# Six wide input products of a mixer: from fp32 to three passes of high and low parts, with modulation rows in two pieces between the low parts

## The chip, the cores and the metric

One core of a Trainium2 chip runs the whole program. The metric is the device time of one execution in microseconds. TensorE (PE; PEld is its weight load), VectorE (DVE), ScalarE (ACT), GpSimd (POOL) and SyncE (SP, which issues nearly all DMAs) run their own instruction streams and meet at semaphores.

## The reference, cut to what matters

The program is a long chain of transformer-like blocks on 256 tokens of width 1024. The change touches one stage, the input side of the first mixer (`even_mixer`):

```
sh, sc, g = adaln(c, e_mod_mix_w[j], e_mod_mix_b[j])
h = rmsnorm(x, e_norm_mix[j]) * (1.0 + sc) + sh
...
fq, fk, fv, ff, gq, gk, gv, gg, glr = jnp.split(h @ w_in, cuts, axis=-1)
...
sh, sc, g = adaln(c, e_mod_ffn_w[j], e_mod_ffn_b[j])
```

`h @ w_in` is (256 x 1024) by (1024 x 3096). Beside it the kernel computes modulation rows of later blocks, `silu(c) @ w + b`, from the same stream of weights.

## The kernel before

**Units.** Weights come in units: one unit is a set of two slots of the buffer `ring` (2 x 1 MB for 1024 rows by 2 x 256 columns) with two PSUM banks. There are three sets (`SETS`), used in turn. SP loads unit n only when `unit_done` says that unit n - 3 has been used by TensorE (`freed`), and it goes through the units strictly in order; the two loads of a unit end on `slot_full`.

**The stage `even_in`** has 13 units. Unit 0 is narrow (8 and 16 columns). Units 1, 3, 5, 7, 9, 11 (`MIX_AT`) are the six wide input units; I call them mix 0 to mix 5. Units 2, 4, ..., 12 (`EF_AT`) carry modulation weights; I call them mod 0 to mod 5. So mod i + 1 (unit 2i + 4) is loaded into the set that mix i (unit 2i + 1) leaves, and mix i + 2 into the set that mod i leaves.

**TensorE** goes mix 0, mod 0, mix 1, the small decay product, mod 1, mix 2, mod 2, and so on to mod 5. A mix unit is 32 fp32 matmuls of 128x128 weights by 256 columns (each is two records in the trace), by `wide` (L1269, output by column) or `tokens_first` (L1307, by token). A mod unit is only four one-column matmuls against ones (`mod_ef`, L1369), since VectorE has already multiplied the eight row blocks by silu(c) and added them (`products_in_place`, L3179 for the first, which waits for both slots of the unit, and L3182 for the other seven).

**ScalarE** copies each finished mix unit out of PSUM (`store` L2595, `store_tokens` L2609) and computes the soft gates. **VectorE** also turns the gates into decays (L3457 to L3471, then `raw` L3481).

**Products by parts.** Later stages already take fp32 products in three fp32r passes. ScalarE rounds the weights of a slot to fp32r in another place (`high_part`, L2460, one instruction for 128x2048, signals `w_high`); VectorE subtracts that from the slot and leaves the low part in the slot (`low_part`, L3298, `w_low`); TensorE then multiplies high by high, low by high and high by low (L1397, L1401 and L1405 in `even_ffn`, eight matmuls in each row, one record each). `half_done` says that the first slot of a unit has been used.

Of the kernel before, what the change touches and what calls it, by code (L numbers as in the profile page):

```python
# [13 lines left out]
P = 128  # L14
D = 1024
T = 256
# [53 lines left out]
def program(nc, A, out, stages=ORDER):  # L70
# [478 lines left out]
    def high_area(first, n):  # L549
        return store_area_r[:, first * T:(first + n) * T].rearrange("p (k t) -> p k t", t=T)  # L550
# [50 lines left out]

    EF_GATES = GU_UNITS if has("even_ffn") else 0
    AFTER_MOE = "ffn1_0" if has("moe") else None
# [92 lines left out]

    EVEN_SLOTS = 2 * GU_UNITS if has("even_ffn") else 0
    EVEN_H = KD if has("even_ffn") else 0

# [57 lines left out]
    with nc.Block() as block:  # L757
# [476 lines left out]
        def _(pe):  # L1234
# [148 lines left out]
            def even_ffn():  # L1383
                norm("ef")
                first = base["even_ffn"]

                def gate_up(u, i):
                    banks_free(u)
                    for s in range(2):
                        high, low = even_high(s), slot(u, s, KD, rounded=True)  # L1390
                        pe.wait_ge(w_high, 2 * i + s + 1)
                        for t in range(2):
                            out, cols = banks[2 * u.r + s][:, t * T:(t + 1) * T], slice(t * P, (t + 1) * P)
                            for k in range(KD):
                                if i == s == t == 0:
                                    pe.wait_ge(h_high, k + 1)
                                mm(out, high[:, k, cols], h_hi[:, k, :], start=(k == 0), stop=False)  # L1397
                            if t == 0:
                                pe.wait_ge(w_low, 2 * i + s + 1)
                            for k in range(KD):  # L1400
                                mm(out, low[:, k, cols], h_hi[:, k, :], start=False, stop=False)  # L1401
                            for k in range(KD):
                                if i == s == t == 0:
                                    pe.wait_ge(h_low, k + 1)
# [203 lines left out]
            def even_mixer():  # L1608
# [21 lines left out]
                mod_ef(1)  # L1630
                wide(Unit(first + MIX_AT[3]), KD, h)
                mod_ef(2)
                wide(Unit(first + MIX_AT[4]), KD, h)
                mod_ef(3)
                tokens_first(Unit(first + MIX_AT[5]), KD, by_token)
                mod_ef(4)
                wide(Unit(first + MIX_AT[6]), KD, h)
                mod_ef(5)
# [750 lines left out]
        def _(se):  # L2389
# [29 lines left out]
            def even_ffn():  # L2419
# [7 lines left out]
                for i in range(GU_UNITS):  # L2427
                    if i + 1 < GU_UNITS:
                        se.wait_ge(half_done, i + 1)
# [226 lines left out]
            def even_mixer():  # L2656
                input_in()
                norm("em")
                st = "even_in"
                se.wait_ge(cols_in, 16 * (len(COL_LOADS) + 3))  # L2660
                u = Unit(base[st])
# [15 lines left out]
                tally.wait(se)  # L2677
                activation(soft[:, 0:2, :], soft[:, 0:2, :], ACT.Ln, bias=ones[:, 0:1]).then_inc(soft_ready, 1)
                store(st, MIX_AT[3], lambda s: flat(fox_q[:, 2 * s:2 * s + 2, :]), scale=DH ** -0.5, with_ef=1)
                store(st, MIX_AT[4], lambda s: flat(fox_k[:, 2 * s:2 * s + 2, :]), with_ef=1)  # L2680

                se.wait_ge(query_raw, 1)
# [7 lines left out]
                for i in range(3):  # L2690
                    key(i)
                store_tokens(st, MIX_AT[5], fox_v, with_ef=1)
                store(st, MIX_AT[6], lambda s: flat(gla_g[:, 2 * s:2 * s + 2, :]), ACT.Silu, with_ef=1)
                for i in range(3, NB):
# [443 lines left out]
        def _(ve):  # L3138
# [49 lines left out]
            def even_low(i, s):  # L3188
                low_part(gate_unit(i), s, KD, even_high(s), 2 * i)

# [36 lines left out]
            def even_ffn():  # L3227
# [12 lines left out]
                for k in range(KD):  # L3240
                    ve.wait_ge(h_high, k + 1)
                    nc.vector.scalar_tensor_tensor(out=h_lo[:, k, :], in0=hT[:, k, :], scalar=shift(k), in1=as_f(h_hi[:, k, :]),
                                                   op0=ALU.add, op1=ALU.subtract).then_inc(h_low, 1)
# [195 lines left out]
            def even_mixer():  # L3439
                norm("em")  # L3440

                def products(i):
                    products_in_place(Unit(base["even_in"] + EF_AT[i]), mod_count(IN_MODS + i))

                products(0)
                ve.wait_ge(soft_ready, 1)
# [6 lines left out]

                products(1)
                ve.wait_ge(soft_ready, 2)
                x = gate_in[:, 0:2, :]
                tally.up(nc.vector.tensor_scalar(x, x, 0.0, None, ALU.min))  # L3457
                tally.wait(ve)
                tally.up(nc.vector.tensor_tensor(x, x, soft[:, 0:2, :], ALU.subtract))
                tally.wait(ve)  # L3460
                for j in range(2):
                    tally.up(nc.vector.tensor_tensor_scan(gla_b[:, j, :], ones[:, :], gate_in[:, j, :], 0.0, ALU.mult, ALU.add))
                tally.wait(ve)

                FLOOR = -60.0 * 16.0
                for j in range(2):
                    b = gla_b[:, j, :].rearrange("p (n t) -> p n t", t=GB)
                    tally.up(nc.vector.tensor_tensor(gla_qd[:, j, :].rearrange("p (n t) -> p n t", t=GB), b,
                                                     b[:, :, GB // 2 - 1:GB // 2].to_broadcast([P, NB, GB]), ALU.subtract))
                tally.wait(ve)  # L3470
                nc.vector.tensor_scalar(gla_qd[:, :, :], gla_qd[:, :, :], -FLOOR, None, ALU.min).then_inc(query_raw, 1)  # L3471
                products(2)
                products(3)

# [15 lines left out]

                for i in range(3):
                    raw(i)
# [724 lines left out]
```

## Time and profile before

| | us |
|---|---|
| median of 3 runs | 2916.94 (2914.49 to 2916.98) |
| the profiled execution, its own time | 2913.85 |
| its span, first to last instruction | 2912.1 |

The page gives PE busy 2800.3 us of the span, DVE 1945.6, ACT 1404.2 and POOL 278.3. An engine's busy time is a sum over the whole program, while the change lies in the first 5% of it, so the stage has to be read by itself: who waits there, and for what. The stage of the wide units runs from 48.6 to 142.0 us.

### The profile page before, as it was taken

The numbers are of one execution on the slowest core, as the hardware profiler recorded it, in microseconds if no ns is written. First come the engines' busy times: TensorE is split into PE (matmuls) and PEld (weight loads), VectorE is DVE, ScalarE is ACT, GpSimd is POOL, SyncE is SP. The second block draws the span as 40 slices with busy tenths as digits, with TensorE's granted clock in tenths as the row PEclk, the third lists the DMA queues.
The fourth block names the chain that finished last, engine by engine and source line by source line (L and its number), as shares of the span: only waits on it lengthen the run. The fifth ranks groups of instructions, "written<-read, shape, count | busy, mean of one in ns | idle before, by whom it ended". The sixth has DMA issues, their size and how long they took to land.

```text
span 2912.1 us, 39687 instructions
## 1 busy us (share of the span) xinstructions
PE 2800.3 (96%) x15590; PEld 2433.1 (84%) x15591; DVE 1945.6 (67%) x2310; ACT 1404.2 (48%) x1569; POOL 278.3 (10%) x248
## 2 busy tenths in 40 slices
PE   6999999989999999999998999999999999999999
PEld 5879988877888888888877888888888988996888
DVE  5466552548888888987544763785577577585765
ACT  2233323217777776776433551343555455435544
POOL 0015732300000000000001000002100010020000
PEclk8999999989999999999999999999999999999999
DMA  8836773368999999997553564333356456572553
GB/s 264 272 120 206 227 232 102 95 202 296 333 345 370 334 342 345 367 335 276 188 188 100 190 192 139 122 117 115 123 188 216 141 171 199 165 202 73 188 181 113
DMA packets 504828, 609.70 MB, mean 209 GB/s; under 512 B 50201, under 2 KB 371836, under 8 KB 504700
## 3 DMA queue, kind: packets, MB, share of 16 engines
q1 hardware_dynamic: 502224, 606.82, 62.8%
q8 instruction: 94, 1.54, 0.2%
q10 hardware_dynamic: 2476, 1.06, 0.1%
q14 instruction: 34, 0.28, 0.0%
HBM read 605.75 MB, written 1.05 MB: 208 GB/s over the span
## 4 chain that ended last, share of the span: by engine, by line
PE 83%; DVE 6%; DMA 4%; ACT 3%; issue 3%; POOL 1%; SPq 0%; DVEq 0%; ACTq 0%; POOLq 0%
PE bank L1452 14%; PE bank L2049 7%; PE bank L1456 7%; PE bank L1444 7%; PE bank L1895 4%; PE bank L1899 4%; PE bank L1908 4%; PE bank L1269 4%; PE bank L1808 3%; PE bank L1321 3%; PE bank L1957 2%; PE bank L1948 2%; PE bank L1949 2%; DMA ring<-in_o_exp_down 2%; PE bank L1401 1%
## 5 line engine op out<-in xcount | busy, mean ns | idle before, releaser
L3298 DVE TENSOR_TENSOR ring_r<-ring,store_area_r 128x2048 fp32r<-128x2048 f32 (+1 forms) x344 | 809.8, 2382 | 191.2 <-ACT store_area_r L2460 188.1
L2460 ACT ACTIVATE store_area_r<-ring 128x2048 fp32r<-128x2048 f32 (+1 forms) x344 | 670.9, 1974 | 229.1 <-PE bank L1456 57.2
L1452 PE MATMUL bank<-hT_sq_r,store_area_r 128*128 128x512 f32 x1376 | 347.9, 395 | 0.5 <-DVE ring_r L3298 0.5
L1452 PEld LDWEIGHTS bank<-hT_sq_r,store_area_r 128*128 128x128 f32 x1376 | 249.5, 190 | 45.8 <-DVE ring_r L3298 0.8
L2049 PE MATMUL bank<-hT,ring 128*128 128x256 f32 x1024 | 229.9, 380 | 0.0
L3757 DVE TENSOR_TENSOR ring_r<-ring,store_area_r 128x3072 fp32r<-128x3072 f32 x64 | 195.0, 3087 | 49.7 <-ACT store_area_r L2893 49.7
L2049 PEld LDWEIGHTS bank<-hT,ring 128*128 128x128 f32 x1024 | 190.8, 190 | 27.1 <-issue 3.1
L1456 PEld LDWEIGHTS bank<-hT_sq_r,ring_r 128*128 128x128 f32 x1376 | 187.9, 191 | 13.5
L2893 ACT ACTIVATE store_area_r<-ring 128x3072 fp32r<-128x3072 f32 x64 | 163.5, 2560 | 73.8 <-DMA ring<-in_o_exp_down 57.3
L1195 POOL TENSOR_TENSOR silu_g<-silu_g 128x768 f32<-128x768 f32 (+2 forms) x14 | 29.9, 2137 | 1707.2 <-ACT silu_g L2472 1338.2
L1456 PE MATMUL bank<-hT_sq_r,ring_r 128*128 128x256 f32 x1376 | 191.9, 282 | 0.0
L1895 PE MATMUL bank<-store_area_r 128*128 128x512 f32 x624 | 160.5, 399 | 4.1 <-issue 4.1
L1899 PE MATMUL bank<-store_area_r 128*128 128x512 f32 x624 | 155.1, 391 | 0.0
L1908 PE MATMUL bank<-ring_r,store_area_r 128*128 128x512 f32 x616 | 152.4, 389 | 0.0
L1899 PEld LDWEIGHTS bank<-store_area_r 128*128 128x128 f32 x624 | 117.9, 189 | 25.2
L1895 PEld LDWEIGHTS bank<-store_area_r 128*128 128x128 f32 x624 | 115.1, 190 | 28.0 <-issue 4.3
L1908 PEld LDWEIGHTS bank<-ring_r,store_area_r 128*128 128x128 f32 x616 | 115.2, 188 | 23.7
L1452 PE MATMUL bank<-act_both_r,store_area_r 128*128 128x512 f32 x528 | 126.2, 391 | 3.2 <-DVE act_both_r L3342 3.2
L1948 PE MATMUL bank<-store_area_r,act_r 128*128 128x512 f32 x308 | 122.4, 398 | 0.0
L1949 PE MATMUL bank<-store_area_r,act_r 128*128 128x512 f32 x308 | 120.3, 390 | 0.0
L3182 DVE SCALAR_TENSOR_TENSOR ring<-ring,csil 128x512 f32<-128x512 f32 x140 | 115.2, 823 | 4.9
L1452 PEld LDWEIGHTS bank<-act_both_r,store_area_r 128*128 128x128 f32 x528 | 97.0, 188 | 23.5 <-DVE act_both_r L3342 4.9
(563 smaller groups left out, 4774.4 us busy)
## 6 DMA issues: line engine op xcount, KB each, us to landing
ring<-in_o_exp_gate SPq DMA_DIRECT2D x88, 1024.0 KB, 7.2
ring<-in_o_exp_up SPq DMA_DIRECT2D x88, 1024.0 KB, 7.2
ring<-in_ffn_w_gu SPq DMA_DIRECT2D x88, 1024.0 KB, 6.6
ring<-in_o_exp_down SPq DMA_DIRECT2D x32, 1536.0 KB, 8.7
ring<-in_ffn_w_down SPq DMA_DIRECT2D x32, 1408.0 KB, 8.7
ring<-in_o_exp_down SPq DMA_DIRECT2D x32, 1280.0 KB, 11.5
ring<-in_ssd_w_in SPq DMA_DIRECT2D x32, 1024.0 KB, 7.2
ring<-in_e_mod_mix_w SPq DMA_DIRECT2D x12, 1024.0 KB, 9.2
```

Of the source, the lines that this page charges most:

```text
L1444: i = mm(out, w(k), x(k), start=(p == k == 0), stop=(p == 2 and k == blocks - 1))
L1452: mm(bank[:, :], w_hi(k), x_both(k), start=(start and k == blocks[0]), stop=False)
L1456: i = mm(bank[:, half * T:(half + 1) * T], w_lo(k), x_hi(k), start=False, stop=(stop and k == blocks[-1]))
L1895: mm(out, xg_r[:, k, HIGH], moe_cols(i, k, high_place(u)), start=(k == 0), stop=False)
L1899: mm(out, xg_r[:, k, LOW], moe_cols(i, k, high_place(u)), start=False, stop=False)
L1908: ins = mm(moe_out(banks[2 * u.r], i), xg_r[:, k, HIGH], moe_low(u, i, k), start=False, stop=(k == KD - 1))
L1948: mm(out, act_r[:, k, HIGH], high[:, j, :], start=(k == 0), stop=False)
L1949: mm(out, act_r[:, k, LOW], high[:, j, :], start=False, stop=False)
L2049: ins = mm(dense_bank(i, s)[:, half * T:(half + 1) * T], slot(u, s, KD)[:, k, half * P:(half + 1) * P], h(k), start=(k == 0), stop=(k == K ...
L2460: activation(dst, slot(u, s, kk), ACT.Copy).then_inc(w_high, 1)
L3298: nc.vector.tensor_tensor(slot(u, s, kk, rounded=True), slot(u, s, kk), as_f(high), ALU.subtract).then_inc(w_low, 1)
L3757: vec.tensor_tensor(down_wide(u, rounded=True)[:, j:j + m, :], down_wide(u)[:, j:j + m, :], as_f(down_high_wide(i)[:, j:j + m, :]), ALU.su ...
```

## The change

All six mix units take three passes instead of fp32 products: 96 fp32r matmuls each. ScalarE makes the high part of each slot (`high`, two per unit, and one of the inputs h), into `act` for slot 0 and the store area for slot 1. VectorE makes the low part of h and of each slot, and the modulation rows are cut in two pieces of four row blocks, laid between the two low parts of a unit (`lows`). The decays move behind the second low part of mix 2. The loads and their order are as before.

```diff
-    EVEN_SLOTS = 2 * GU_UNITS if has("even_ffn") else 0
-    EVEN_H = KD if has("even_ffn") else 0
+    MIX_SLOTS, MIX_H, MIX_HALVES = (12, KD, 6) if has("even_in") else (0, 0, 0)
+    EVEN_SLOTS = MIX_SLOTS + (2 * GU_UNITS if has("even_ffn") else 0)
+    EVEN_H = MIX_H + (KD if has("even_ffn") else 0)
...
+    mix_high = lambda s: high_area(56, KD) if s else act_r[:, 0:KD, :]
+    mix_lo = high_area(64, KD)
+    mix_unit = lambda i: Unit(base["even_in"] + MIX_AT[i + 1])
...
-                by_token = lambda k, a: hT[:, k, a * P:(a + 1) * P]
-                wide(Unit(first + MIX_AT[1]), KD, h)
+                def mix(i, tokens=False):
+
+                    u = mix_unit(i)
+                    banks_free(u)
+                    for s in range(2):
+                        high, low = mix_high(s), slot(u, s, KD, rounded=True)
+                        pe.wait_ge(w_high, 2 * i + s + 1)
+                        for t in range(2):
+                            out, part = banks[2 * u.r + s][:, t * T:(t + 1) * T], slice(t * P, (t + 1) * P)
+                            for p, (w, x) in enumerate(((high, h_hi), (low, h_hi), (high, mix_lo))):
+                                if p == 0 and i == s == t == 0:
+                                    pe.wait_ge(h_high, KD)
+                                if p == 1 and t == 0:
+                                    pe.wait_ge(w_low, 2 * i + s + 1)
+                                if p == 2 and i == s == t == 0:
+                                    pe.wait_ge(h_low, KD)
+                                for k in range(KD):
+                                    ins = mm(out, *((x[:, k, part], w[:, k, :]) if tokens else (w[:, k, part], x[:, k, :])),
+                                             start=(p == k == 0), stop=(p == 2 and k == KD - 1))
+                        ins.then_inc(unit_done if s else half_done, 1)
+                mix(0)
                 mod_ef(0)
-                tokens_first(Unit(first + MIX_AT[2]), KD, by_token)
+                mix(1, tokens=True)
                 pe.wait_ge(evac, first + 1)
                 pe.wait_ge(cols_in, 16 * (len(COL_LOADS) + 3))
                 for j in range(2):
                     i = mm(bank_x[:, j * T:(j + 1) * T], gla_w2[:, j * P:(j + 1) * P], soft[0:16, 2, :], start=True, stop=True)
                 i.then_inc(decay_ps, 1)
                 mod_ef(1)
-                wide(Unit(first + MIX_AT[3]), KD, h)
+                mix(2)
...
+                def high(i, s):
+                    if i >= 1:
+                        se.wait_ge(*((unit_done, mix_unit(i - 1).at(1)) if s else (half_done, i)))
+                    high_part(mix_unit(i), s, KD, mix_high(s))
+
+                se.wait_ge(h_ready, KD)
+                activation(h_hi[:, :, :], hT[:, :, :], ACT.Copy).then_inc(h_high, KD)
+                for s in range(2):
+                    high(0, s)
...
+                high(1, 0)
                 store(st, MIX_AT[1], lambda s: flat(gla_q if s == 0 else gla_k), with_ef=1)
+                high(1, 1)
+                high(2, 0)
                 store_tokens(st, MIX_AT[2], gla_v, with_ef=1)
+                high(2, 1)
...
+                def products(i, rows):
+                    products_in_place(Unit(base["even_in"] + EF_AT[i]), mod_count(IN_MODS + i), rows)
+
+                def lows(i, between=None):
+                    low_part(mix_unit(i), 0, KD, mix_high(0), 2 * i)
+                    products(i, range(KD // 2))
+                    low_part(mix_unit(i), 1, KD, mix_high(1), 2 * i)
+                    if between:
+                        between()
+                    products(i, range(KD // 2, KD))
+
+                ve.wait_ge(h_high, KD)
+                nc.vector.tensor_tensor(mix_lo, hT[:, :, :], as_f(h_hi[:, :, :]), ALU.subtract).then_inc(h_low, KD)
+                lows(0)
...
-                products(1)
-                ve.wait_ge(soft_ready, 2)
...
-                products(2)
-                products(3)
+                lows(1)
...
+                def decays():
+                    ve.wait_ge(soft_ready, 2)
+                    x = gate_in[:, 0:2, :]
...
+                lows(2, decays)
+                lows(3)
+                lows(4)
+                lows(5)
                 ve.wait_ge(query_exp, 1)
                 nc.vector.scalar_tensor_tensor(out=gla_qd[:, :, :], in0=gla_qd[:, :, :], scalar=DH ** -0.5, in1=gla_q[:, :, :],
                                                op0=ALU.mult, op1=ALU.mult).then_inc(query_ready, 1)
-                products(4)
-                products(5)
```

`high_part`, `low_part` and `products_in_place` are those described above; `EF_AT` gives the mod units.

Three places in the streams. First VectorE, from the gates' small instructions behind mod 0 on. Before, the eight instructions of mod 1 (here by their kind, 1 and 7) follow at once, then the decays:

```order
L3452 SCALAR_TENSOR_TENSOR store_area<-ones,store_area 8x256
L3179 TENSOR_SCALAR ring<-ring,csil 128x2x256
L3182 SCALAR_TENSOR_TENSOR ring<-ring,csil 128x2x256 x7
L3457 TENSOR_SCALAR store_area<-store_area 128x512
L3459 TENSOR_TENSOR store_area<-store_area 128x512
```

In the changed kernel, from the same instruction on, the rows are those of `lows(1)` (`ring_r<-ring,act_r` is the low part of slot 0, `ring_r<-ring,store_area_r` that of slot 1) and the beginning of `lows(2)`:

```order
L3505 SCALAR_TENSOR_TENSOR store_area<-ones,store_area 8x256
L3341 TENSOR_TENSOR ring_r<-ring,act_r 128x2048
L3222 TENSOR_SCALAR ring<-ring,csil 128x2x256
L3225 SCALAR_TENSOR_TENSOR ring<-ring,csil 128x2x256 x3
L3341 TENSOR_TENSOR ring_r<-ring,store_area_r 128x2048
L3225 SCALAR_TENSOR_TENSOR ring<-ring,csil 128x2x256 x4
L3341 TENSOR_TENSOR ring_r<-ring,act_r 128x2048
L3222 TENSOR_SCALAR ring<-ring,csil 128x2x256
```

The low part of mix 1's second slot now stands behind the first four product instructions of mod 1, the first of which (L3222) waits for both slots of the mod unit.

Second, TensorE between mod 0 and mod 1. Before:

```order
L1369 MATMUL bank<-ones,ring 128x1 x4
L1307 MATMUL bank<-ring,hT 128x256 x32
L1628 MATMUL bank<-store_area,gla_w 128x256 x2
L1369 MATMUL bank<-ones,ring 128x1 x4
```

In the changed kernel the first slot's six passes of mix 1 come first (they read alike but for `act_r` in place of `store_area_r`), and then these, the second slot's:

```order
L1642 MATMUL bank<-store_area_r,hT_sq_r 128x256 x8
L1642 MATMUL bank<-ring_r,hT_sq_r 128x256 x8
L1642 MATMUL bank<-store_area_r 128x256 x8
L1642 MATMUL bank<-store_area_r,hT_sq_r 128x256 x8
L1642 MATMUL bank<-ring_r,hT_sq_r 128x256 x8
L1642 MATMUL bank<-store_area_r 128x256 x8
L1651 MATMUL bank<-store_area,gla_w 128x256 x2
L1373 MATMUL bank<-ones,ring 128x1 x4
```

Of the second slot's 48 matmuls only the first eight (high by high) can run before the low part; the other 40 stand behind the wait for `w_low`.

Third, ScalarE around the copies of mix 0 and mix 1. Before they stood side by side:

```order
L2595 ACTIVATE store_area<-bank 128x512 x2
L2609 ACTIVATE store_area<-bank 128x2x256 x2
```

Now the high parts stand between them (`act_r<-ring` is slot 0, `store_area_r<-ring` slot 1):

```order
L2483 ACTIVATE act_r<-ring 128x2048
L2618 ACTIVATE store_area<-bank 128x512 x2
L2483 ACTIVATE store_area_r<-ring 128x2048
L2483 ACTIVATE act_r<-ring 128x2048
L2632 ACTIVATE store_area<-bank 128x2x256 x2
```

The high part of a unit's slot 0 is ahead of the copy of the unit before it, that of slot 1 behind it.

## Rows read from the trace of the kernel before

**Rows 1.** The page: busy time by engine, and the chain by engine.

```profile
PE 2800.3 (96%) x15590; PEld 2433.1 (84%) x15591; DVE 1945.6 (67%) x2310; ACT 1404.2 (48%) x1569; POOL 278.3 (10%) x248
...
PE 83%; DVE 6%; DMA 4%; ACT 3%; issue 3%; POOL 1%; SPq 0%; DVEq 0%; ACTq 0%; POOLq 0%
```

**Rows 2.** Busy time in the stage: PE, PEld, DVE, ACT, POOL, granted clock, DMA.

```profile
48.60:142.00 93.40, 90.42 (x437) 78.70 (x436) 39.87 (x63) 21.79 (x33) 0.00 (x0) 1.00 0.79 253
```

**Rows 3.** Timeline of PE: start, us, engine, line, [idle before <- releaser].

```profile
48.57 14.08 PE L1269 MATMUL bank<-hT,ring 128*128 128x256 f32 x64
...
63.30 14.06 PE L1307 MATMUL bank<-ring,hT 128*128 128x256 f32 x64
...
140.96 1.05 PE L1369 MATMUL bank<-ones,ring 128*128 128x1 f32 x8 [2.16 <-DVE ring L3182]
```

**Rows 4.** Waits of the stage: us in total, times, longest.

```profile
DVE ring L3179 <- DMA ring<-in_e_mod_ffn_w: 26.0, 3, 11.6
```

**Rows 5.** Timeline of SP's DMA issues.

```profile
62.69 1.26 SPq L766 DMA_DIRECT2D ring<-in_e_mod_mix_w  x2
63.99 4.18 SPq L766 DMA_DIRECT2D ring<-in_e_w_in  x2
...
93.35 1.26 SPq L766 DMA_DIRECT2D ring<-in_e_mod_ffn_w  x2
...
108.65 1.26 SPq L766 DMA_DIRECT2D ring<-in_e_mod_ffn_w  x2
...
124.12 15.96 SPq L766 DMA_DIRECT2D ring<-in_e_mod_ffn_w  x6
```

**Rows 6.** Timeline of DVE: the first product instruction of four mod units.

```profile
71.67 0.48 DVE L3179 TENSOR_SCALAR ring<-ring,csil 128x512 f32<-128x512 f32 x1 [16.87 <-DMA ring<-in_e_mod_mix_w]
...
103.07 0.49 DVE L3179 TENSOR_SCALAR ring<-ring,csil 128x512 f32<-128x512 f32 x1 [9.48 <-DMA ring<-in_e_mod_ffn_w]
...
117.27 0.49 DVE L3179 TENSOR_SCALAR ring<-ring,csil 128x512 f32<-128x512 f32 x1 [4.87 <-DMA ring<-in_e_mod_ffn_w]
...
134.90 0.49 DVE L3179 TENSOR_SCALAR ring<-ring,csil 128x512 f32<-128x512 f32 x1 [11.64 <-DMA ring<-in_e_mod_ffn_w]
```

**Rows 7.** Timeline of ACT: the last step of the inputs h.

```profile
38.84 3.30 ACT L2417 ACTIVATE hT<-hT,mods 128x256 f32<-128x256 f32 x8 [14.27 <-DVE hT L3167]
```

**Rows 8.** The critical chain in order of time: start, us, what.

```profile
39.49 9.16 PE bank L1619 x32
...
233.22 1.71 PE bank L1401 x8
...
238.80 0.96 PE bank L1397 x8
```

**Rows 9.** Groups by form, of `even_ffn` (first two) and of this stage.

```profile
L3298 DVE TENSOR_TENSOR ring_r<-ring,store_area_r 128x2048 fp32r<-128x2048 f32 x21 | 52.1, 2480 | 37.7 <-ACT store_area_r L2460 37.7
...
L2460 ACT ACTIVATE store_area_r<-ring 128x2048 fp32r<-128x2048 f32 x20 | 38.2, 1910 | 42.5 <-PE bank L1405 42.5
...
L3182 DVE SCALAR_TENSOR_TENSOR ring<-ring,csil 128x512 f32<-128x512 f32 x42 | 31.6, 752 | 1.5
...
L3179 DVE TENSOR_SCALAR ring<-ring,csil 128x512 f32<-128x512 f32 x5 | 2.4, 485 | 42.8 <-DMA ring<-in_e_mod_ffn_w 26.0 <-DMA ring<-in_e_mod_mix_w 16.9
```

**Rows 10.** Timeline of PE where it comes back from a wait.

```profile
229.94 3.29 PE L1397 MATMUL bank<-hT_sq_r,store_area_r 128*128 128x256 f32 x8 [3.57 <-ACT hT_sq_r L2415]
```

**Rows 11.** Windows around that wait: PE busy, granted clock, DMA share, GB/s.

```profile
228.00:230.00 2.00, 0.06 (x1) 1.00 1.10 348
...
234.00:236.00 2.00, 2.00 (x16) 0.78 0.66 210
...
236.00:238.00 2.00, 2.00 (x19) 1.00 0.01 2
```

**Rows 12.** Timeline of DVE: first and last step of the decays, and `raw`.

```profile
83.96 0.43 DVE L3457 TENSOR_SCALAR store_area<-store_area 128x512 f32<-128x512 f32 x1 [6.29 <-ACT store_area L2678]
...
87.25 0.43 DVE L3471 TENSOR_SCALAR store_area<-store_area 128x512 f32<-128x512 f32 x1
...
108.98 1.26 DVE L3481 TENSOR_SCALAR store_area<-store_area 128x128 f32<-128x128 f32 x6
```

More of the change, by code:

```diff
@@ L599, in ffn_gain @@
         return NORMS[name][1](k)
-    EF_GATES = GU_UNITS if has("even_ffn") else 0
+    EF_GATES = (6 if has("even_in") else 0) + (GU_UNITS if has("even_ffn") else 0)
     AFTER_MOE = "ffn1_0" if has("moe") else None
@@ L1390, in gate_up @@
                         high, low = even_high(s), slot(u, s, KD, rounded=True)
-                        pe.wait_ge(w_high, 2 * i + s + 1)
+                        pe.wait_ge(w_high, MIX_SLOTS + 2 * i + s + 1)
                         for t in range(2):
@@ L1395, in gate_up @@
                                 if i == s == t == 0:
-                                    pe.wait_ge(h_high, k + 1)
+                                    pe.wait_ge(h_high, MIX_H + k + 1)
                                 mm(out, high[:, k, cols], h_hi[:, k, :], start=(k == 0), stop=False)
                             if t == 0:
-                                pe.wait_ge(w_low, 2 * i + s + 1)
+                                pe.wait_ge(w_low, MIX_SLOTS + 2 * i + s + 1)
                             for k in range(KD):
@@ L1630, in even_mixer @@
                 mod_ef(1)
-                wide(Unit(first + MIX_AT[3]), KD, h)
+                mix(2)
                 mod_ef(2)
-                wide(Unit(first + MIX_AT[4]), KD, h)
+                mix(3)
                 mod_ef(3)
-                tokens_first(Unit(first + MIX_AT[5]), KD, by_token)
+                mix(4, tokens=True)
                 mod_ef(4)
-                wide(Unit(first + MIX_AT[6]), KD, h)
+                mix(5)
                 mod_ef(5)
@@ L2428, in even_ffn @@
                     if i + 1 < GU_UNITS:
-                        se.wait_ge(half_done, i + 1)
+                        se.wait_ge(half_done, MIX_HALVES + i + 1)
                         high(i + 1, 0)
@@ L2678, in even_mixer @@
                 activation(soft[:, 0:2, :], soft[:, 0:2, :], ACT.Ln, bias=ones[:, 0:1]).then_inc(soft_ready, 1)
+                high(3, 0)
                 store(st, MIX_AT[3], lambda s: flat(fox_q[:, 2 * s:2 * s + 2, :]), scale=DH ** -0.5, with_ef=1)
+                high(3, 1)
+                high(4, 0)
                 store(st, MIX_AT[4], lambda s: flat(fox_k[:, 2 * s:2 * s + 2, :]), with_ef=1)
+                high(4, 1)
                 se.wait_ge(query_raw, 1)
@@ L2691, in even_mixer @@
                     key(i)
+                high(5, 0)
                 store_tokens(st, MIX_AT[5], fox_v, with_ef=1)
+                high(5, 1)
                 store(st, MIX_AT[6], lambda s: flat(gla_g[:, 2 * s:2 * s + 2, :]), ACT.Silu, with_ef=1)
@@ L3188, in even_low @@
             def even_low(i, s):
-                low_part(gate_unit(i), s, KD, even_high(s), 2 * i)
+                low_part(gate_unit(i), s, KD, even_high(s), MIX_SLOTS + 2 * i)
             def mod_out(u, n, bank):
@@ L3240, in even_ffn @@
                 for k in range(KD):
-                    ve.wait_ge(h_high, k + 1)
+                    ve.wait_ge(h_high, MIX_H + k + 1)
                     nc.vector.scalar_tensor_tensor(out=h_lo[:, k, :], in0=hT[:, k, :], scalar=shift(k), in1=as_f(h_hi[:, k, :]),
@@ L3452, in even_mixer @@
                 tally.up(nc.vector.tensor_tensor_scan(fox_cum[0:8, 0, :], ones[0:8, :], x, 0.0, ALU.mult, ALU.subtract))
-                products(1)
-                ve.wait_ge(soft_ready, 2)
[L3456 to L3471, printed above, removed]
-                products(2)
-                products(3)
+                lows(1)
                 def raw(i):
@@ L3489, in key @@
                     nc.vector.tensor_tensor(kd, kd, gla_k[:, :, 0:w], ALU.mult).then_inc(key_ready, 1)
-                for i in range(3):
-                    raw(i)
+                FLOOR = -60.0 * 16.0
+                def decays():
+                    ve.wait_ge(soft_ready, 2)
+                    x = gate_in[:, 0:2, :]
+                    tally.up(nc.vector.tensor_scalar(x, x, 0.0, None, ALU.min))
+                    tally.wait(ve)
+                    tally.up(nc.vector.tensor_tensor(x, x, soft[:, 0:2, :], ALU.subtract))
+                    tally.wait(ve)
+                    for j in range(2):
+                        tally.up(nc.vector.tensor_tensor_scan(gla_b[:, j, :], ones[:, :], gate_in[:, j, :], 0.0, ALU.mult, ALU.add))
+                    tally.wait(ve)
+                    for j in range(2):
+                        b = gla_b[:, j, :].rearrange("p (n t) -> p n t", t=GB)
+                        tally.up(nc.vector.tensor_tensor(gla_qd[:, j, :].rearrange("p (n t) -> p n t", t=GB), b,
+                                                         b[:, :, GB // 2 - 1:GB // 2].to_broadcast([P, NB, GB]), ALU.subtract))
+                    tally.wait(ve)
+                    nc.vector.tensor_scalar(gla_qd[:, :, :], gla_qd[:, :, :], -FLOOR, None, ALU.min).then_inc(query_raw, 1)
+                    for i in range(3):
+                        raw(i)
+                lows(2, decays)
+                lows(3)
+                lows(4)
+                lows(5)
                 ve.wait_ge(query_exp, 1)
```

5 lines of the change are left out of this document (1 added, 4 removed).

## The prediction

> **What bounds the kernel now.** I read the page first: TensorE is busy for 96% of the span and the chain that ended last is TensorE for 83% [rows 1]. So time saved on TensorE counts, if nothing else takes its place in that stretch. Next the windows of the stage: from 48.6 to 142.0 us, 93.4 us, TensorE is busy for 90.42 and the granted clock is 1.00; VectorE is busy for only 39.87 and ScalarE for 21.79 [rows 2]. By busy time the stage is bound by TensorE, and there seems to be room for 12 low parts and 13 high parts.
>
> Then the timelines, to see who is close behind. A wide unit with its mod unit takes 14.7 us from start to start (48.57 to 63.30) [rows 3]. The loads of mod i + 1 are issued in the moment in which mix i ends: TensorE's first unit ends at 39.49 + 9.16 = 48.65 [rows 8], mix 0 at about 62.65, since SP issues at 62.69 [rows 5]. They have landed when VectorE's first product, which waited for them, starts: 62.69 to 71.67, 93.35 to 103.07, 108.65 to 117.27, 124.12 to 134.90 [rows 5, 6]. So a load takes 8.98, 9.72, 8.62 and 10.78 us. VectorE stands 26.0 us in three of these waits [rows 4]; today nothing that TensorE needs soon is queued behind it, except the modulation row itself. The eight products take 0.49 + 7 x 0.75 = 5.8 us [rows 9], and 9 to 11 + 6 us is just about the length of a mix unit: at the end TensorE waits 2.16 us for them [rows 3]. The view that decides is therefore not busy time but this ring: mix ends, load, VectorE, TensorE. It is as long as TensorE's own work already now.
>
> **The change part by part.**
>
> *Passes in place of fp32 products.* A mix unit takes 62.65 - 48.65 = 14.0 us now. Eight fp32r matmuls of the same shape take 0.96 us at full clock [rows 8], so 12 rows of eight take 11.5 us. By TensorE alone the six units would save 6 x 2.5 = 15 us, and the 3 us of waits with them if VectorE kept up.
>
> *High parts on ScalarE.* 1.91 us each [rows 9]. That of slot 1 waits until the unit before has ended and its copy, so it is there some 3 us after that end, while TensorE first works on slot 0 for 5.8 us. Nothing is late. Priced at nothing; were it exposed, it would be 1.9 us a unit.
>
> *Prologue.* h is ready at 38.84 + 3.30 = 42.1 [rows 7]. High part of h until 44.1, its low part until 46.5, low part of slot 0 until 48.9, four products until 51.7, low part of slot 1 until 54.1. TensorE needs the first at 48.65 + 1.0 and the last at 48.65 + 5.8 + 1.0 = 55.4. It is all under the narrow unit (9.16 us [rows 8]) and the first slot. Mix 0 then ends at 48.65 + 11.5 = 60.2, which is 2.5 us earlier than now.
>
> *Low parts and products in pieces on VectorE.* This is the step that counts. A low part took 2.48 us on average in the later stage [rows 9]; I take 2.4, as GpSimd, which is busy there, does nothing here [rows 2]. The order is: low part of slot 0, four products of mod i, low part of slot 1, four products. The first product waits for the mod unit's two slots, whose load is issued only when mix i - 1 ends. So the low part of slot 1 of mix i, on which 40 of the unit's 96 matmuls wait, now stands behind a load that starts when mix i - 1 ends. Counted from that end:
> - the load, for mod 1 to mod 5: 8.98, then for mod 2 the mean of the three like it (its own can't be read, VectorE came to it late), 9.1, then 9.72, 8.62, 10.78 [rows 5, 6]: 47.2 us, 9.44 on average;
> - four products, 0.49 + 3 x 0.75 = 2.8 us with small gaps [rows 9];
> - the low part, 2.4 us;
> - semaphores, 0.1 us;
> - 40 matmuls, 5 x 0.96 = 4.8 us at full clock [rows 8].
>
> TensorE meanwhile does mod i - 1, slot 0 and the first eight of slot 1: it stands still from about 1.0 + 5.8 + 1.0 = 7.8 us after the end to 14.7, for 6.9 us. What the clock does then shows where TensorE came back from a wait of 3.57 us at 229.94 [rows 10]: the granted clock was 1.00 at the end of the wait, and then eight matmuls took 1.71 us instead of 0.96, 0.214 each [rows 8]; it came back within the window from 234 to 236, of mean 0.78, so at about 234.9 [rows 11], after 5.0 us of work at the lower of the two levels, 1.2 GHz. For a wait of 6.9 us I take the same: 5.0 us at 0.214 are 23 matmuls, and 17 at 0.12 are 2.0, so the 40 take 7.0 us. Bounds: 4.8 (no fall) and 8.6 (all low). Behind them come slot 0 and more, whose clock doesn't matter: they have 6.9 us to spare.
>
> From one mix end to the next: 9.44 + 2.8 + 2.4 + 0.1 + 7.0 = 21.7 us, where the kernel before needs about 15.2 (mix 0 ends at 62.65; mod 5 starts at 140.96 after a 2.16 us wait, so mix 5 ended at 138.8 [rows 3]). Mix 5 ends at 60.2 + 5 x 21.7 = 168.9 and mod 5 at 170.0, against 140.96 + 1.05 = 142.0 now: **28 us later**.
>
> The Trainium skill ("TensorE: Matmul & The Clock Gate", HAM oscillation) says that bursts of matmuls parted by DMA waits each start at the low clock; it speaks against this change, and without that rule the sum would be 5 x 2.2 = 11 us less. For the load, the skill ("DMA: Bandwidth & Descriptors", Where 436 GB/s comes from, and Latency and other measured facts) gives about 358 GB/s and about 2 us of fixed cost, an estimate of 7.9 us for these 2.1 MB; by it the delay would be 20 us and not 28. The rows of this very stage are longer, and they decide.
>
> *Decays behind the low part of mix 2.* They last from 83.96 to 87.7, and six `raw` 1.26 us [rows 12], 5.0 in all, and the last four products of mod 2 come 3.0 us behind. So mod 2 is ready 8.0 us after that low part, and mix 2 ends 7.0 after it: mod 2 waits 1.0 us. That delays the start of mix 3, which has 6.9 us to spare, and not the load of mod 3, issued when mix 2 ends. Price nothing; without that cover 1 us. The weights of mix i + 2 are issued behind mod i and follow the mod loads by 1.3 us as now [rows 5]; even at twice 9 us after the end of mix i, the high part of slot 0 is done at 19.9 and the low part at 22.3, while TensorE wants them at 22.7 and 23.7, behind mix i + 1 and its mod unit. Not late either, though the low part by little.
>
> *After the stage* the order is as before: the end of mod 5 releases the same steps, later.
>
> **The sum.** 2913.85 + 28 = 2942 us against the profiled execution. Its time is 3.1 us below the median of the runs, 2916.94; I leave 2942. In it five periods cost 6.5 us each, 32.5 in all; the 2.5 us won at mix 0 and the last wait of 2.2 us, which goes away, are taken off.
>
> **The rivals.**
> 1. *The clock hardly falls in the waits.* For it: 7 us of standing still follow on 14 us of dense work. Against it: [rows 10, 11], a wait half as long. The tail is 4.8, a period 19.5, the delay 17 us: 2931. With the shortest load, 8.62, and a low part of 2.3 in all five: 18.6 a period, +12, 2926. Chance 0.17.
> 2. *The chain is slower yet.* All 40 matmuls at the low clock (8.6) and loads like the longest (10.78): 24.7 a period, +43, 2957. Either alone gives +36 (tail) or +35 (loads). Chance 0.12 for +33 and more.
> 3. *Faster: the load is hidden after all and TensorE bounds.* Then 48.65 + 6 x (11.5 + 0.9) + 1 for the decay product = 124 instead of 142: 18 us less, 2896. It decides at the landing: the low part would have to be done by 7.6 us after the mix end, so the load must land within 2.4 us of its issue. The shortest seen is 8.62. Chance 0.03.
> 4. *No change.* A period of 16.2 us (15.2, and a fifth each of the 2.5 won at the start and the 2.2 at the end) needs a landing within 3.9 us if the clock falls or 6.1 if it doesn't. Nothing in the rows speaks for it; it would also come about if the products' first wait didn't hold back the low part, and then the rival above takes over. Chance 0.03.
>
> **How the numbers follow.** The forecast's chance is 0.65, over 2934 to 2947. With the parts of rivals 1 and 2 that lie next to it, 2929 to 2952 leaves out the shortest loads without a fall of the clock, the far end of rival 2, and rivals 3 and 4: 2 in 10. Under 0.2% (6 us) a measurement of this kernel can't tell from no change. Faster 0.03, same 0.03, slower 0.94.
>
> **What the changed kernel's profile would show.** In the stage, about 28 us longer, TensorE's busy time stays at some 87 us (69 of passes, 11 of lost clock, 7 of the small ones), with five idle stretches of about 7 us, ended by VectorE's low part of slot 1 (L3341) on the matmuls of the second pass (L1642); none in mix 0. VectorE waits at L3222 for the DMA 6 us or more in each of five units, and the two loads before it are issued at each mix end. The granted clock is 0.5 behind each wait and returns within some 5 us. The passes take 0.96 us in dense stretches. If the loads landed well before VectorE came to L3222, or if TensorE's waits ended on ScalarE's high parts, the reasoning is wrong. The stages behind mod 5 should last as long as before.

## The result, and the profile after

| | us |
|---|---|
| before, median of 4 runs | 2915.72 |
| changed, median of 4 runs | 2936.84 (2935.41 to 2937.26) |
| ratio | 1.0074, 95% interval 1.0061 to 1.0088 |
| the changed kernel's profiled execution, its span | 2936.55, 2934.8 |

The changed kernel is 21 us slower, 0.7%. On its page TensorE is busy for less time than before, in a longer span (the chain has the same shares within a point) [rows 1]:

```profile
PE 2797.5 (95%) x15782; PEld 2440.1 (83%) x15783; DVE 1973.0 (67%) x2323; ACT 1427.6 (49%) x1582; POOL 279.2 (10%) x248
...
PE 84%; DVE 6%; DMA 3%; ACT 3%; issue 3%; POOL 1%; SPq 0%; DVEq 0%; ACTq 0%; POOLq 0%
```

The stage by windows (columns as in [rows 2]), now up to 166.0 us, which is 1.2 us short of its end:

```profile
48.60:166.00 117.40, 86.23 (x620) 84.20 (x620) 64.71 (x77) 37.91 (x40) 0.00 (x0) 0.85 0.61 197
```

117.4 us instead of 93.4, of which TensorE is busy for 86.2 instead of 90.4, and the mean granted clock is 0.85 instead of 1.00. So TensorE stands still for 31 us instead of 3. The waits of the changed kernel from 42 to 166 us say on what:

```profile
DVE ring L3222 <- DMA ring<-in_e_mod_ffn_w: 39.0, 4, 11.0
...
PE bank L1642 <- DVE ring_r L3341: 30.9, 5, 6.7
...
DVE ring L3222 <- DMA ring<-in_e_mod_mix_w: 9.4, 1, 9.4
```

Five waits of TensorE for a low part, 30.9 us in all; and ahead of each of them VectorE waits at the first product of a mod unit for its load. TensorE's timeline has all five: the first eight matmuls of slot 1, then the pass that needs the low part, with the idle time before it in brackets [rows 3]:

```profile
66.96 1.12 PE L1642 MATMUL bank<-store_area_r,hT_sq_r 128*128 128x256 f32 x8
74.76 2.07 PE L1642 MATMUL bank<-ring_r,hT_sq_r 128*128 128x256 f32 x8 [6.68 <-DVE ring_r L3341]
...
96.07 2.07 PE L1642 MATMUL bank<-hT_sq_r,ring_r 128*128 128x256 f32 x8 [5.92 <-DVE ring_r L3341]
...
117.67 2.08 PE L1642 MATMUL bank<-hT_sq_r,ring_r 128*128 128x256 f32 x8 [5.56 <-DVE ring_r L3341]
...
138.80 2.07 PE L1642 MATMUL bank<-ring_r,hT_sq_r 128*128 128x256 f32 x8 [6.36 <-DVE ring_r L3341]
...
159.68 2.08 PE L1642 MATMUL bank<-hT_sq_r,ring_r 128*128 128x256 f32 x8 [6.39 <-DVE ring_r L3341]
...
166.24 0.95 PE L1373 MATMUL bank<-ones,ring 128*128 128x1 f32 x8
```

One turn of the ring is best read in the chain (start, us, what). From the end of mix 0 to that of mix 1 it goes through SP, the load, four products, a low part and 40 matmuls:

```profile
60.50 0.55 SPq L770
...
61.10 8.46 DMA ring<-in_e_mod_mix_w
...
69.65 0.50 DVE ring L3222
...
72.50 2.21 DVE ring_r L3341
...
74.76 6.55 PE bank L1642 x40
81.33 0.55 SPq L770
```

This turn takes 20.8 us. The loads in all five turns, read as in [rows 5, 6] from the issue (60.50, 81.33, 103.76, 124.88, 145.72) to the first product, are 9.15, 9.63, 8.81, 8.82 and 8.86 us long. VectorE's rows for two of them:

```profile
69.65 0.49 DVE L3222 TENSOR_SCALAR ring<-ring,csil 128x512 f32<-128x512 f32 x1 [9.43 <-DMA ring<-in_e_mod_mix_w]
...
154.58 0.48 DVE L3222 TENSOR_SCALAR ring<-ring,csil 128x512 f32<-128x512 f32 x1 [10.61 <-DMA ring<-in_e_mod_ffn_w]
```

The windows around the first wait show the clock (TensorE's busy time stands behind the window's length, the granted clock behind that of all engines):

```profile
68.00:70.00 2.00, 0.07 (x1) 0.00 (x0) 0.35 (x1) 0.00 (x0) 0.00 (x0) 1.00 1.10 351
70.00:72.00 2.00, 0.00 (x0) 0.00 (x0) 1.89 (x4) 0.00 (x0) 0.00 (x0) 0.83 1.10 348
72.00:74.00 2.00, 0.00 (x0) 0.00 (x0) 2.00 (x2) 1.35 (x1) 0.00 (x0) 0.50 1.07 338
...
76.00:78.00 2.00, 2.00 (x11) 2.00 (x11) 1.93 (x4) 0.00 (x0) 0.00 (x0) 0.50 0.00 0
78.00:80.00 2.00, 2.00 (x18) 2.00 (x18) 1.93 (x1) 0.00 (x0) 0.00 (x0) 0.96 0.00 0
```

Its means put the fall at about 71.3, some 3 us into the wait, and the return at about 78.2, 3.4 us after the matmuls came back. Read in the same way, the return comes 6.0, 4.9, 4.2 and 3.8 us after the matmuls in the other four turns. Mod 5 ends at 166.24 + 0.95 = 167.2, 25.2 us later than before. At the end of the program 22.7 us of that are left (2934.8 against 2912.1).

### The profile page after: what moved, and what is told of

The parts are those of the page before. It is cut to its first block, busy times and chain, and to the rows that moved or that the text cites. A ratio compares the mean times of both kernels' runs of the same rounds, so it can differ in the third digit from the quotient of the medians.

```text
span 2934.8 us, 40109 instructions
## 1 busy us (share of the span) xinstructions
PE 2797.5 (95%) x15782; PEld 2440.1 (83%) x15783; DVE 1973.0 (67%) x2323; ACT 1427.6 (49%) x1582; POOL 279.2 (10%) x248
## 3 DMA queue, kind: packets, MB, share of 16 engines
HBM read 605.75 MB, written 1.05 MB: 207 GB/s over the span
## 4 chain that ended last, share of the span: by engine, by line
PE 84%; DVE 6%; DMA 3%; ACT 3%; issue 3%; POOL 1%; SPq 0%; DVEq 0%; ACTq 0%; POOLq 0%
PE bank L1456 13%; PE bank L2072 7%; PE bank L1460 7%; PE bank L1448 7%; PE bank L1918 4%; PE bank L1922 4%; PE bank L1931 4%; PE bank L1273 4%; PE bank L1325 3%; PE bank L1831 3%; PE bank L1980 2%; PE bank L1971 2%; PE bank L1972 2%; PE bank L1642 2%; DMA ring<-in_o_exp_down 1%
## 5 line engine op out<-in xcount | busy, mean ns | idle before, releaser
L3341 DVE TENSOR_TENSOR ring_r<-ring,store_area_r 128x2048 fp32r<-128x2048 f32 (+1 forms) x350 | 822.5, 2379 | 190.9 <-ACT store_area_r L2483 188.1
L2483 ACT ACTIVATE store_area_r<-ring 128x2048 fp32r<-128x2048 f32 (+1 forms) x350 | 682.2, 1973 | 229.3 <-PE bank L1460 57.1
L1199 POOL TENSOR_TENSOR silu_g<-silu_g 128x768 f32<-128x768 f32 (+2 forms) x14 | 29.9, 2134 | 1702.4 <-ACT silu_g L2495 1331.9
```

What stands on the lines that cost most here:

```text
L2483: activation(dst, slot(u, s, kk), ACT.Copy).then_inc(w_high, 1)
L3341: nc.vector.tensor_tensor(slot(u, s, kk, rounded=True), slot(u, s, kk), as_f(high), ALU.subtract).then_inc(w_low, 1)
```

## The experiments

All but half_mod_loads are compared with the kernel before by runs on the same chip. Where nothing else is said, an experiment is the changed kernel with one edit. "The stage ends" means the end of mod 5's matmuls: 142.0 us before, 167.2 in the changed kernel. A mod row is the few small matmuls of a mod unit, and the tail is the 40 matmuls of a mix unit behind the low part of its second slot.

**lows_first.** Both low parts ahead of the products.

```diff
 low_part(mix_unit(i), 0, KD, mix_high(0), 2 * i)
-products(i, range(KD // 2))
 low_part(mix_unit(i), 1, KD, mix_high(1), 2 * i)
 if between:
     between()
-products(i, range(KD // 2, KD))
+products(i, range(0, KD))
```

> Both low parts of a unit stand ahead of all eight products of its mod unit on VectorE; nothing else is changed. Theory A (the low part of slot 1 queued behind the products' wait for the load is what costs): TensorE no longer stands still inside a mix unit; what is left is the old ring, load 9.1 + eight products 5.9 + mod row 0.9 = 16 us from the end of one mix to the end of the mod row after the next, so that two units take about 27.5 us. The stage ends at about 131 to 137 us of the span instead of 167, and the time is 2900 to 2908 us, faster than both kernels. Rival B (the extra work of high and low parts on ScalarE and VectorE is too much whatever its order): the second slot still waits for its low part, and the time stays above 2925 us. Rival C (loads get longer when TensorE goes faster, the queue has more to do): loads of 12 us or more, time about 2915 us.

Measured: ratio 0.9985 (0.9975 to 0.9995), median 2910.17 us. The stage ends at 138.7. No matmul waits for a low part any more; what is left are waits of the mod rows for their products. TensorE's timeline of this kernel has them:

```profile
76.13 1.05 PE L1373 MATMUL bank<-ones,ring 128*128 128x1 f32 x8 [2.45 <-DVE ring L3225]
...
94.09 1.30 PE L1373 MATMUL bank<-ones,ring 128*128 128x1 f32 x8 [3.73 <-DVE ring L3225]
...
123.46 1.05 PE L1373 MATMUL bank<-ones,ring 128*128 128x1 f32 x8 [2.77 <-DVE ring L3225]
137.72 0.95 PE L1373 MATMUL bank<-ones,ring 128*128 128x1 f32 x8
```

The same instructions in another order end the stage 28.5 us earlier, and by the ratios the time is 24 to 26 us less. That is the mechanism of theory A; rival B needed over 2925 us, and rival C loads of 12 us or more (the mod loads that VectorE waited for took 8.7 to 9.8 us). Its numbers were too good: the stage ends at 138.7 and not at 131 to 137, and 2910.17 us lies outside 2900 to 2908. The longest wait is the one before mod 2, at 94.09, since the decays stand ahead of its eight products. VectorE itself waited there for ScalarE's gates, which come behind the high parts of mix 2:

```profile
83.23 0.43 DVE L3529 TENSOR_SCALAR store_area<-store_area 128x512 f32<-128x512 f32 x1 [2.75 <-ACT store_area L2715]
```

**one_ahead.** Only the first product, the one that waits for the load, ahead of the low part.

```diff
-products(i, range(KD // 2))
+products(i, range(1))
 low_part(mix_unit(i), 1, KD, mix_high(1), 2 * i)
 if between:
     between()
-products(i, range(KD // 2, KD))
+products(i, range(1, KD))
```

> Only the first product of each mod unit, which waits for its load, stays ahead of the low part of slot 1; the other seven go behind it. Theory A in its two parts (wait for the load, then what VectorE does before the low part): three products of 0.79 us leave the chain of each of five units, 5 x 2.36 = 11.8 us less, 2925 us, and TensorE still stands still for 3 to 4.5 us in each unit, ended by the low part; if that shorter wait leaves the clock up, up to 10 us more come off, 2915 us. Rival (only the number of instructions ahead of the low part counts, not the load): 2910 us or less, since 3 of 4 products are gone.

Measured: ratio 1.0035 (1.0020 to 1.0049), median 2923.71 us. The stage ends at 156.2, 11.0 us earlier than in the changed kernel, for 11.8 expected. TensorE waits 3.50 to 5.53 us in four of the units; in the fifth, mix 3, it doesn't wait for the low part, but mod 2 ahead of it waits 2.63 us for its products. The clock falls here too, so the 10 us more that it might have given back did not come: the first eight matmuls behind even the shortest of the four waits take 2.08 us, as behind a long one. The rival (2910 us or less) is out.

```profile
93.34 2.08 PE L1642 MATMUL bank<-hT_sq_r,ring_r 128*128 128x256 f32 x8 [3.50 <-DVE ring_r L3341]
```

**all_ahead.** All eight products ahead of it.

```diff
-products(i, range(KD // 2))
+products(i, range(8))
 low_part(mix_unit(i), 1, KD, mix_high(1), 2 * i)
 if between:
     between()
-products(i, range(KD // 2, KD))
```

> All eight products of a mod unit stand ahead of the low part of slot 1. Theory A (everything that VectorE does between the landing and that low part is on the chain): four more products of 0.79 us in each of five units, 15.7 us more, and some 1.6 us once at mix 0, where the low part now ends at about 57 us while TensorE wants it at 55.4: the stage ends at about 184 instead of 167 us and the time is 2953 us. Rival (the period is set by the load alone, VectorE has slack): 2937 us as before. With lows_first and one_ahead this gives a series in the number of products ahead: 0, 1, 4, 8.

Measured: ratio 1.0127 (1.0111 to 1.0143), median 2952.51 us. The stage ends at 186.1, 18.9 us later than with four ahead, for 17.3 expected, and mix 0 now has a wait too, of 1.83 us. TensorE's other five waits grow to 9.15 to 10.96 us:

```profile
80.41 2.08 PE L1642 MATMUL bank<-ring_r,hT_sq_r 128*128 128x256 f32 x8 [10.96 <-DVE ring_r L3341]
```

The series of 0, 1, 4 and 8 products ahead gives stage ends of 138.7, 156.2, 167.2 and 186.1 us. The first product alone, 0.5 us of work and one wait, costs 17.5 us; the other seven together 29.9.

**half_mod_loads.** Half the bytes in each mod unit (the second edit is shown by what it comes to, the choice of the row block).

```diff
 for s, src in enumerate(mod_columns(IN_MODS + EF_AT.index(at))):
-    load(u, s, src)
+    load(u, s, src[:, 0:KD // 2, :])
...
-nc.vector.scalar_tensor_tensor(out=w(0), in0=w(k), ...
+nc.vector.scalar_tensor_tensor(out=w(0), in0=w(1 + (k - 1) % 3), ...
```

> The mod units of this stage load only the first four of eight row blocks (half the bytes), and the products take rows 1 to 3 again in place of 4 to 7, so the modulation rows made from them are other numbers; instructions and waits are as many. Later stages that depend on these rows can take another time, so the stage itself is read. Theory A (the load's own length is on the chain): a load takes about 6 instead of 9.05 us and the stage ends some 5 x 3 = 15 us earlier, at about 152 us instead of 167. Rival (VectorE's own work sets the period, and the load only seems to be waited for): the end stays at 165 to 167 us.

Measured: the stage ends at 146.5, 20.7 us earlier. The loads take 6.25, 5.35, 5.48, 5.30 and 5.24 us, 3.5 less each, which is 17.7 in five turns. SP's and VectorE's timelines for the second:

```profile
78.99 0.92 SPq L770 DMA_DIRECT2D ring<-in_e_mod_ffn_w  x2
```

```profile
84.34 0.49 DVE L3222 TENSOR_SCALAR ring<-ring,csil 128x512 f32<-128x512 f32 x1 [6.78 <-DMA ring<-in_e_mod_ffn_w]
```

Most of the other 3 us come from mix 2: its wait for the low part is only 1.64 us, the matmuls behind it ran at full rate, and its tail took 5.1 us instead of 7.67. Behind the wait of 3.78 us they ran slowly from the start. Behind those of 2.84 and 2.78 us only the first eight ran at full rate; then the clock fell, and these tails took 6.55 us, hardly less than the 6.90 and 6.72 of the changed kernel.

```profile
72.39 2.07 PE L1642 MATMUL bank<-ring_r,hT_sq_r 128*128 128x256 f32 x8 [3.78 <-DVE ring_r L3341]
...
89.45 1.22 PE L1642 MATMUL bank<-hT_sq_r,ring_r 128*128 128x256 f32 x8 [1.64 <-DVE ring_r L3341]
...
122.25 1.22 PE L1642 MATMUL bank<-ring_r,hT_sq_r 128*128 128x256 f32 x8 [2.84 <-DVE ring_r L3341]
123.30 1.64 PE L1642 MATMUL bank<-store_area_r 128*128 128x256 f32 x8
```

So the load's length is on the chain, and its rival is out. In four of the five turns TensorE still waits for the low part behind it; in mix 3 it doesn't, as mod 2 ahead of it waits 2.78 us for its own products. One execution was taken of this one, and its whole time isn't compared.

**filled_wait.** 48 spare matmuls where TensorE stands still.

```diff
 if p == 1 and t == 0:
+    if s == 1 and i > 0:
+        for n in range(6 * KD):
+            mm(bank_sum[:, T:2 * T], high[:, n % KD, 0:P], h_hi[:, n % KD, :], start=(n == 0), stop=(n == 6 * KD - 1))
     pe.wait_ge(w_low, 2 * i + s + 1)
```

> The changed kernel with 48 spare matmuls of 128x128 by 256 (into unused columns of a bank) behind the first eight matmuls of slot 1 in mix 1 to mix 5, in the time in which TensorE stands still. Theory A with the clock term as in the prediction: the spare work is hidden, the granted clock stays at 1.00, the 40 matmuls take 4.8 us instead of the 6.5 to 7.7 measured, 10 to 11 us less in the five units: 2926 us. Rival (the clock behind a wait costs nothing that counts, or VectorE holds up the later passes too): 2937 us as before. Rival (spare work isn't hidden): 5 x 5.8 us slower, 2966 us.

Measured: ratio 1.0069 (1.0050 to 1.0089), median 2932.49 us. By its whole time it can't be told from the changed kernel, whose two ratios are 1.0074 and 1.0068, so the stage has to decide. It ends at 162.7, 4.5 us earlier, not 11. The tails went as expected: in all five units the granted clock is 1.00 behind the spare work, the passes start 0.96 us apart (the first two 1.05), and the tail takes 5.0 to 5.1 us, about 10 us less in all. In mix 1, where the wait is longer than the spare work, that work is hidden too:

```profile
67.64 5.92 PE L1640 MATMUL bank<-hT_sq_r,store_area_r 128*128 128x256 f32 x48
75.09 1.22 PE L1645 MATMUL bank<-ring_r,hT_sq_r 128*128 128x256 f32 x8 [1.53 <-DVE ring_r L3344]
76.14 1.12 PE L1645 MATMUL bank<-store_area_r 128*128 128x256 f32 x8
...
101.90 1.87 PE L1373 MATMUL bank<-ones,ring 128*128 128x1 f32 x8 [2.34 <-DVE ring L3228]
...
112.47 5.92 PE L1640 MATMUL bank<-hT_sq_r,store_area_r 128*128 128x256 f32 x48
118.23 1.12 PE L1645 MATMUL bank<-hT_sq_r,ring_r 128*128 128x256 f32 x8
```

The rest was given back at mod 2 and mix 3, whose turn takes 23.6 us instead of 21.1. With mix 2's tail shorter, mod 2 has to wait for its products behind the decays (2.34 us, at 101.90), and mix 3 starts late and at the low clock. VectorE came to the products at 108.22 there, so with 5.1 us for four of them and the low part its low part was ready at 113.3, but the spare work lasts until 118.2: 4.9 us of it are exposed. So the clock term stands, read at the five tails; for the whole time the run was too blunt, its filler being of one length.

**hidden_work.** 4.6 us more for VectorE in each of five units, ahead of the landing.

```diff
 low_part(mix_unit(i), 0, KD, mix_high(0), 2 * i)
+if i:
+    for n in range(4):
+        tally.wait(ve)
+        tally.up(nc.vector.tensor_tensor(std[:, :], flat2(hT[:, 0:4, :]), flat2(hT[:, 4:8, :]), ALU.subtract))
 products(i, range(KD // 2))
```

> The changed kernel with four spare subtractions of 128x1024 (about 1.15 us each, 4.6 us, into a scratch tile) on VectorE between the low part of slot 0 and the first product in units 1 to 5, in the time in which it waits for the load. Theory A (only what stands behind the landing counts): nothing changes, 2937 us, as VectorE waits 6.5 to 11 us there. Rival B (VectorE has too much to do in this stage): 5 x 4.6 = 23 us slower, 2960 us.

Measured: ratio 1.0071 (1.0054 to 1.0088), median 2935.48 us, against 2934.65 for the changed kernel on the same chip (next). The added work came to 5.0 us in each unit. VectorE's wait for the load is shorter by it (11.04 us at this place in the changed kernel), and the stage ends at 168.2, which is 1.0 us later than in the changed kernel's first profile and 2.3 later than in its second:

```profile
92.35 0.48 DVE L3222 TENSOR_SCALAR ring<-ring,csil 128x512 f32<-128x512 f32 x1 [6.07 <-DMA ring<-in_e_mod_ffn_w]
```

25 us of extra work cost about 1 us of the median, within the spread of the runs, while in all_ahead 15.7 us moved between the landing and the low part cost 18.9 us of the stage. That settles rival B: it isn't the amount of work on VectorE.

**changed_again.** The changed kernel once more.

> The changed kernel itself, on the same chip as the others of this call: 22 us slower than the fp32 kernel, the stage's end at 167 us within 1 us, under every theory. It gives the spread of the loads (8.8 to 9.6 us) and of the clock's return from one chip to the next.

Measured: ratio 1.0068 (1.0052 to 1.0084), median 2934.65 us, which is 18.7 us slower than the kernel before and not 22; the stage ends at 165.8, so it is 1.4 us off the first profile and a little outside the 1 us expected. The loads take 8.6 to 9.8 us. One changed kernel against itself thus differs by about 1.4 us in the stage, and smaller differences between experiments say nothing.

**lows_first_decays_later.** As lows_first, with the decays between the two low parts of mix 3.

```diff
 low_part(mix_unit(i), 0, KD, mix_high(0), 2 * i)
-products(i, range(KD // 2))
+if between:
+    between()
 low_part(mix_unit(i), 1, KD, mix_high(1), 2 * i)
-if between:
-    between()
-products(i, range(KD // 2, KD))
+products(i, range(KD))
...
-lows(2, decays)
-lows(3)
+lows(2)
+lows(3, decays)
```

> Both low parts ahead of all eight products, as in lows_first, and the decays moved from mix 2 (where the mod row came 3.7 us late behind them) to mix 3, between its two low parts. Theory A (VectorE's order around the landing sets the rest): the 3.7 us wait before mod 2 goes and none takes its place, the stage ends at about 135 us, some 7 us before that of the fp32 kernel; ratio to it 0.9975 to 0.998, and 3 to 4 us faster than lows_first. Rival (the ring load + products + mod row gives the time back at the next mod row): stage end at 138.7 as in lows_first, ratio 0.9985.

Measured: ratio 0.9968 (0.9955 to 0.9981), median 2907.1 us against 2915.91 of the kernel before: faster than both kernels. The stage ends at 137.2 instead of 138.7. So the gain over lows_first in the stage is 1.5 us and not 3.7, no more than the spread just named: the wait before mod 2 is gone, but two later mod rows wait for their products, where only one did:

```profile
76.32 1.86 PE L1373 MATMUL bank<-ones,ring 128*128 128x1 f32 x8 [2.56 <-DVE ring L3225]
...
105.97 1.05 PE L1373 MATMUL bank<-ones,ring 128*128 128x1 f32 x8 [2.15 <-DVE ring L3225]
...
135.80 1.41 PE L1373 MATMUL bank<-ones,ring 128*128 128x1 f32 x8 [2.37 <-DVE ring L3225]
```

That is in part the rival of its expectation. Of its 9 us in the whole time the stage accounts for 4.8; where the others are isn't shown, and the interval of its ratio reaches down to 5.5 us.

## Why the prediction was right

It said 2942 (2929 to 2952) and slower; measured are 2936.84. As a difference it said 28 us, and 21.1 were measured: the forecast was built on an execution of 2913.85, 1.9 us below the median that counts, and that hides a part of the miss. The profiled executions differ by 25.2 us at the stage's end and by 22.7 at the last instruction. The five waits, their line, their releaser and their absence in mix 0 came as listed. By its steps:

- **The ring.** Right, and shown in both directions: without the product that waits ahead of the low part the slowdown is gone (lows_first), with more products ahead it grows (all_ahead), and the load's length counts in full (half_mod_loads).
- **Load.** 9.44 us expected, 9.05 measured on average: 2 us too much in five turns. The first four lie within 0.9 us of what was taken for each; the fifth, which took 10.78 before, took 8.86 now.
- **Four products and the low part.** 5.2 us, and 0.1 for semaphores; 5.1 in all measured (69.65 to 74.76). Right.
- **The tail of 40 matmuls.** 7.0 expected; 6.55, 7.67, 7.19, 6.90 and 6.72 measured, 7.0 on average. The clock is its cause: in filled_wait the tails took 5.0 to 5.1. But that the mean came out to the tenth is in part luck. The "5.0 us of work at the lower level" that I took from [rows 10, 11] was misread, as the window that I left out there shows (columns as in [rows 11]):

```profile
230.00:232.00 2.00, 1.95 (x6) 0.87 1.11 349
232.00:234.00 2.00, 2.00 (x9) 0.50 1.10 350
```

The clock fell there only at about 231.5, 1.5 us after the matmuls had come back, and was low for 3.4 us. In the changed kernel it stayed low for 3.4 to 6.0 us behind the matmuls' return, about 4.4 on average, and the 40 matmuls at full clock take 5.0 to 5.1 and not 4.8. A low stretch taken too long and a full-clock time taken too short cancelled.
- **Prologue and mix 0.** 60.2 expected, and the mod row behind it starts at 60.31. Right.
- **Decays.** Mod 2 waits 0.17 us instead of 1.0, as mix 2 had the longest tail, and 1.14 in changed_again, where that tail was 1 us shorter; it moves nothing in the changed kernel. As soon as the tail is shorter or all the products stand behind the decays they do cost (2.34 us in filled_wait, 3.73 in lows_first), so "price nothing" held only under that cover.
- **A turn.** 21.7 expected, 21.2 measured ((166.24 - 60.31) / 5). The stage ends 25.2 us later, not 28. Of the difference 2 us are the load term and 1 the four products with the low part.
- **Behind the stage.** "As before" is off by 2.5 us: the distance shrinks from 25.2 to 22.7 over the rest of the program. It doesn't shrink steadily: in the two chains the same product stands 24.3 us apart at 217 us of the changed kernel's span, 27.5 at 588 and 24.2 at 1363. It changes by other amounts in other executions (23.8 to about 21.6 in changed_again), and the cause isn't settled. The medians of the kernel before in the three groups of runs lie within 1.4 us, but single runs of it from 2908.72 to 2920.35.

The rivals: the clock did fall, so the first is out; the slower chain was not seen; that the load is hidden is out, by [rows 5, 6] already; and "no change" is out with a ratio of at least 1.0061. The extra work as such, which I didn't name as a rival of the prediction but tested, isn't the cause either (hidden_work).

## What to carry to other kernels

An engine that works in order passes on the wait at its head to everything behind it: before work is interleaved "to fill gaps", ask when the event comes for which each piece waits, and put first what is ready first and wanted first. Here VectorE was busy for 40 of 93 us before the change, and one misplaced wait of a 0.5 us instruction cost 17.5 us, and with three more instructions behind it 28.5. Where a buffer ring ties a load to the end of earlier work, write the ring down with its durations (load, then each step up to the end that frees the next set) and compare it with the busy engine's own time; they were nearly equal here before the change, so that some 15 us less work on TensorE gave only 4.8 us of the stage in the best order tried.

## What the runs showed of the hardware that I had not expected

The return of TensorE's clock behind a like wait differed from turn to turn. In the changed kernel the tails with the same 40 matmuls took 6.55 to 7.67 us, with waits of 5.56 to 6.68 us before them, and not in their order (5.92 gave the longest, 6.68 the shortest). Nor did the length of a wait tell whether the clock would fall. It stayed at 1.00 behind the waits of 1.64 us in half_mod_loads and 1.83 us in mix 0 of all_ahead. It fell behind that of 2.84 us in half_mod_loads, and in lows_first behind one of 2.45 us that was followed by a mod row: its timeline has the second eight matmuls of mix 2 at 2.00 us instead of 1.12.

```profile
78.41 2.00 PE L1642 MATMUL bank<-hT_sq_r,ring_r 128*128 128x256 f32 x8
```

In changed_again it fell behind a wait of only 1.14 us before mod 2, and not in the wait but at about 107.4, when TensorE had been back at work for 2.7 us. It had been at the low level before, behind the wait of mix 2, until about 100.6.

```profile
104.61 1.05 PE L1373 MATMUL bank<-ones,ring 128*128 128x1 f32 x8 [1.14 <-DVE ring L3225]
...
106.81 1.64 PE L1642 MATMUL bank<-hT_sq_r,ring_r 128*128 128x256 f32 x8
108.25 1.91 PE L1642 MATMUL bank<-store_area_r,act_r 128*128 128x256 f32 x8
```

So the price of a wait has to be read behind it, in the rows of the next matmuls, and not from its length.
